# Products of ones in two waits of TensorE, and a residual that goes pair by pair, in a two-block transformer kernel

## The reference, cut to what matters

```python
h = rmsnorm(x, norm_pre_mix)
m = hgrn2_mixer(h, ...)                  # ends in the projection  o @ w_out
x = x + rmsnorm(m, norm_post_mix)        # the residual ahead of the FFN
h = rmsnorm(x, norm_pre_ffn)
x = x + rmsnorm(conv_ffn(h, ...), norm_post_ffn)
```

## Time and profile before

| what | value |
|---|---|
| median of 3 runs | 2503.98 us (2502.96 to 2504.39) |
| the profiled execution, first to last instruction | 2504.0 us |
| TensorE busy | 2480.6 us, 99% |
| VectorE, ScalarE, GpSimd busy | 1753.6, 1257.8, 29.5 us |
| mean granted clock of TensorE | 0.997 of full |
| HBM traffic | 463.5 MB, 185 GB/s over the span |

### The profile page before, as it was taken

How to read it: one execution, slowest core, us unless ns; L and a number is a source line. 1 busy time by engine, 2 the same in 40 slices (tenths; PEclk the granted TensorE clock), 3 DMA queues, 4 the chain that set the end, 5 groups by cost and what they waited for, 6 DMA issues and landing times.

```text
span 2504.0 us, 38061 instructions
## 1 busy us (share of the span) xinstructions
PE 2480.6 (99%) x15416; PEld 2115.6 (84%) x15416; DVE 1753.6 (70%) x1978; ACT 1257.8 (50%) x1506; POOL 29.5 (1%) x26
## 2 busy tenths in 40 slices
PE   9999999999999999999999999999999999999998
PEld 7888888888888888888888888888888888888886
DVE  6656765668668677675777777775776666777777
ACT  7655344544444444445555555544654444444543
POOL 0000000000000000000000000000000000000000
PEclk9999999999999999999999999999999999999999
DMA  9454545546546546555545454556465565556553
GB/s 381 153 183 152 176 153 193 176 164 223 193 161 231 187 171 211 193 195 183 185 153 185 153 185 153 185 170 195 150 217 185 186 200 187 183 194 198 186 188 127
DMA packets 128239, 465.97 MB, mean 186 GB/s; under 512 B 14368, under 2 KB 14624, under 8 KB 127168
## 3 DMA queue, kind: packets, MB, share of 16 engines
q1 hardware_dynamic: 127920, 463.53, 55.2%
q10 hardware_dynamic: 144, 0.02, 0.0%
HBM read 461.39 MB, written 2.10 MB: 185 GB/s over the span
## 4 chain that ended last, share of the span: by engine, by line
PE 94%; issue 4%; DVE 2%; ACT 0%; DMA 0%; SPq 0%; DVEq 0%; POOL 0%; POOLq 0%
PE job L970 30%; PE job L982 16%; PE job L938 11%; PE job L940 11%; PE job L939 11%; PE job L957 2%; PE job L958 2%; PE job L959 2%; PE att L958 2%; PE att L957 2%; PE att L959 2%; PE att L1177 1%; PE att L998 0%; DVE w_low L1593 0%; PE att L1010 0%
## 5 line engine op out<-in xcount | busy, mean ns | idle before, releaser
L1274 ACT ACTIVATE w_high<-raw 128x1024 fp32r<-128x1024 f32 (+1 forms) x883 | 919.6, 1050 | 733.9 <-PE job L940 292.4
L1593 DVE TENSOR_TENSOR w_low<-raw,w_high 128x1024 fp32r<-128x1024 f32 (+1 forms) x883 | 1047.0, 1212 | 310.5 <-ACT w_high L1274 231.0
L970 PE MATMUL job<-actA,w_high 128*128 128x512 f32 x3328 | 798.3, 391 | 0.1
L970 PEld LDWEIGHTS job<-actA,w_high 128*128 128x128 f32 x3328 | 611.8, 188 | 119.9 <-issue 0.7
L982 PEld LDWEIGHTS job<-actA,w_low 128*128 128x128 f32 x3328 | 426.7, 191 | 16.2
L982 PE MATMUL job<-actA,w_low 128*128 128x256 f32 x3328 | 431.7, 283 | 0.0
L1796 DVE TENSOR_TENSOR slots<-job,slots 128x512 f32<-128x512 f32 x102 | 70.5, 691 | 344.1 <-ACT slots L1466 343.5
L938 PE MATMUL job<-w_high,actB 128*128 128x512 f32 x736 | 288.6, 392 | 2.5 <-DVE w_low L1593 2.0
L939 PE MATMUL job<-w_low,actB 128*128 128x512 f32 x736 | 287.1, 390 | 0.0
L940 PE MATMUL job<-w_high,actB 128*128 128x512 f32 x736 | 287.0, 390 | 0.0
L938 PE MATMUL job<-w_high,actA 128*128 128x512 f32 x576 | 230.9, 401 | 0.0
(11 more groups left out here) (257 smaller groups left out, 1906.0 us busy)
## 6 DMA issues: line engine op xcount, KB each, us to landing
raw<-in_weights SPq DMA_DIRECT2D x855, 512.0 KB, 4.2
M<-in_mem_t SPq DMA_DIRECT2D x8, 256.0 KB, 8.0
slots<-in_mem SPq DMA_DIRECT2D x2, 1024.0 KB, 12.2
M<-in_x_t SPq DMA_DIRECT2D x4, 512.0 KB, 13.8
H<-in_x SPq DMA_DIRECT2D x2, 1024.0 KB, 9.0
out<-H SPq DMA_DIRECT2D x8, 256.0 KB, 3.2
slots<-in_w_small SPq DMA_DIRECT2D x1, 1024.0 KB, 9.7
slots<-in_post_mix_g SPq DMA_DIRECT2D x1, 1024.0 KB, 4.3
```

The lines of the kernel that those rows point to most:

```text
L970: mm = nc.tensor.matmul(J[job.buf][:, x, :], w_high[:, w % AHEAD, cols], act_both[job.act][:, c, :, :].rearrange("p a t -> p (a t)"), star ...
L1274: nc.scalar.activation(w_high[:, s % AHEAD, cols], raw[:, s % RAW_SLOTS, cols], ACT.Copy)\
L1593: nc.vector.tensor_tensor(w_low[:, s % AHEAD, cols], raw[:, s % RAW_SLOTS, cols], w_high[:, s % AHEAD, cols].bitcast(F32), ALU.subtract).t ...
```

## The change

It has three parts. (1) Behind window 0 TensorE does 8 more products of ones (fp32, 128x128), into a PSUM bank that nothing reads until it is written anew. (2) Behind window `end` it does 16 of them, ahead of `h_turn` 0. (3) The four steps from the residual to the FFN's activations are ordered pair by pair: step k does `post_add`, `h_turn` and `h_split` of pieces 2k and 2k+1, where before `post_add` and `h_turn` ran up to two pairs ahead of `h_split`. `m_gain` of quarter 3 moves from step `end + 2` to `end + 3`.

```diff
+FILL = {"second load": 8, "mixer norm": 16}
...
     p.put_early(end, "post_stat")
+    p.put_early(end, "fill", "mixer norm")
-    for step, added, split in ((end, range(0, 4), (0, 1)), (end + 1, (4, 5), (2, 3)), (end + 2, (6, 7), (4, 5)),
-                               (end + 3, (), (6, 7))):
-        if step == end + 2:
+    for step, added, split in ((end, (0, 1), (0, 1)), (end + 1, (2, 3), (2, 3)), (end + 2, (4, 5), (4, 5)),
+                               (end + 3, (6, 7), (6, 7))):
+        if step == end + 3:
             p.put_early(step, "m_gain", j.buf, 3)
...
                     products(w, range(TT)).then_inc(window_done, 1)
+                    if w == 0:
+                        fill("second load")
...
+            def fill(where):
+                for _ in range(FILL[where]):
+                    nc.tensor.matmul(att[:, 3, 0:P], ones[:, :], ones[:, :], start=True, stop=True)
...
+                elif name == "fill":
+                    for kind in ("o_low", "attended", "o_ready"):
+                        wait(pe, n, kind, 0)
+                    fill(*args)
```

More of the change, by code:

```diff
@@ L213 @@
     "hgrn_attend": dict(attended=1),
+    "fill": {},
     "m_part": dict(m_set=1),
```

## The result

The changed kernel takes 2510.13 us (median of 9 runs, 2509.68 to 2511.69), the kernel before 2503.98 us (median of 9). The ratio is 1.0025, with a 95% interval from 1.0016 to 1.0033: 6.15 us slower. The forecast was 2509.7 us, slower, and the new order as the cause. The time is right to 0.4 us, but by luck: two terms of its sum, of 1.6 us each and with opposite signs, stand for falls of the clock that need not be in the median execution, and they cancel.

The account below looks back on a forecast made before the run. The prediction took VectorE to bound the norm, with TensorE following. It summed 2504.0 - 1.6 (second load) + 5.7 (new order) + 1.6 (one fall in the new waits) = 2509.7 us, range 2507.4 to 2512.9.

Parts of the forecast that it names:

- two terms of its sum: Clock terms: -1.6 us for the fall removed at the second load, +1.6 us for one fall in the new waits.
- What bounds the norm: From 1756.4 to 1771.3 us VectorE, not TensorE, works without a gap, and TensorE follows.
- the walk: Step-by-step timing of pieces through VectorE, TensorE and ScalarE at the norm, at full clock: F3's narrow products 5.7 us later.
- The rival in which TensorE bounds the norm: VectorE's order counts for nothing and both fills win a whole fall: 2500.8 us; 5%.
- The new order, +5.7 us: Pair-by-pair order at the norm starts F3's narrow products at 1778.3 against 1772.55: +5.7 us, second fill's gain included.
- Products at the norm: Sixteen products inside TensorE's wait cost nothing at full clock; worth 0.2 us in the old order, within the +5.7 otherwise.
- Products at the second load, -1.6 us: Eight products behind window 0 fill TensorE's wait at no cost and prevent a clock fall: -1.6 us.
- the prediction's upper bound: At the second load, products at half clock would end 1.4 us late: +1.4 us, put aside.
- the rival: First fill wins nothing as the median execution's fall is elsewhere or escaped: 2511.3 us with one new fall; 7%.
- Falls in the new waits, +1.6 us: Five new TensorE waits at the norm bring one clock fall: +1.6 us, bounds 0 and 4.8.

Follow-up runs that it names:

- e3: Both runs of products of ones added to the kernel before, old order of the residual kept: 2504.27 us, ratio 1.0001.
- e10: Only the 16 products of ones at the norm added to the kernel before, old order: 2503.29 us, ratio 0.9997.
- e6: Changed kernel with residual and turns of pieces 4 and 5 put back a step earlier: 2506.92 us, ratio 1.0009 to the kernel before.
- e7: Both runs of products of ones on the kernel before, old order but for the first pair: 2505.86 us, ratio 1.0005.
- e4: Changed kernel plus 24 more products of ones in TensorE's new waits: 2510.4 us, ratio 1.0025 to the kernel before.
- the 3rd trace of the changed kernel: Another profiled execution of the changed kernel, nothing altered: time 2509.13 us, span 2507.3 us.
- e2: Only the new order on the kernel before, no products of ones: 2512.1 us, ratio 1.0033.
- its 2nd and 3rd trace: Two more profiled executions of the kernel before, nothing altered: times 2503.08 and 2503.73 us, spans 2501.3 and 2501.9 us.
- e1: Only the 8 products of ones behind window 0 added to the kernel before: 2504.39 us, ratio 1.0002.
- e9: Another profiled execution of e1, nothing altered: time 2504.21 us, span 2502.4 us.

## Why the prediction was right, and where it was not

**What bounds the norm**: right. VectorE does, shown by e3 and e10 (the fall at the norm taken away, the norm 19.13 and 19.14 us against 19.16) and by e6 and e7, in which only the order of VectorE's and TensorE's steps differs and the norm moves as the walk says. In the new order no single engine is busy throughout: the chain from engine to engine is the bound, and VectorE idles 6.2 us in it. The rival in which TensorE bounds the norm is out.

**The new order, +5.7 us**: right in size and step by step. At full clock it measures +5.69 (e4, and the 3rd trace of the changed kernel). The waits of the wide products and of turn 6 are in the places named: 1.29, 1.50, 1.49, 0.76 and 1.14 us, where the walk has 1.3, 1.5, 1.65, 0.9 and 1.3. (The prediction calls these "1.0 to 1.8 us"; its own times give 0.9 to 1.65.)

**Products at the norm**: right in the old order, nothing to win (e10). Left unpriced by itself in the new order, where it is the part of the change that pays: 1.9 us of norm between e2 and a trace at full clock, and 2512.1 us of e2 against 2510.13. The expectation for e2 gave it 0.3.

**Products at the second load, -1.6 us**: wrong at the median, by a premise that stands in the sum and ahead of the prediction too. "The profiled execution is the median run to 0.1 us" compared a span with times. The time is about 1.8 us more than its span, so the profiled execution was 1.8 us above the median, and what set it apart was the very fall that I then counted as won. Of five profiles without these products (before, its 2nd and 3rd trace, e2, e10) one has the costly fall there, one an earlier and cheaper one, three none. What took the term's place is nought, or up to 1.1 us of loss. The step behind it, that the products cost nothing, failed as well: they end behind the low part of window 1 in six of nine traces, at full clock (11.54 against 11.03 in the changed kernel). The loss by half clock, the prediction's upper bound, is not shown, since all nine profiles with these products had the full clock behind window 0. The Trainium skill, "TensorE: Matmul & The Clock Gate", section "What's actually happening", says that the same kernel meets the clock gate at another phase from run to run. The traces agree: of three executions of the kernel before, one has the fall behind window 1's first products, one in window 0, and one has none there. The prediction cited this and gave the rival 7%.

**Falls in the new waits, +1.6 us**: the mechanism is right and the place too; the price of one is 1.6 us, as said (norm 26.21 against 24.85, and 0.25 more behind it, where the rest is 731.72 against 731.47 us). It comes in two of three profiles, and not in e2, which has the same waits. How much of it is in the median is open, and the record points both ways. The median time of 2510.13 us is a span of 2508.3. With the fall that leaves a start of 2508.3 - 731.7 - 26.2 = 1750.4 us, earlier than in any of the fourteen traces (1750.71 at the least); without it 1751.95, well among them. And e4, whose profile has no fall, is no faster at the median. By this the median execution goes without the whole price. Yet the mean granted clock is 0.998 in seven of nine executions of the changed kernel, and 0.999 in 7 of 8 of e4 and in 10 of 11 of e3. That speaks for falls in most, though e7's profile, with no fall behind the start, reads 0.998 as well. Falls that lie partly in a wait, and so cost less, would fit both; no trace shows one.

**The sum.** With the right anchor it reads: 2504.0, 0 to +0.3 for the products at the load, +5.7 for the order, and a few tenths at most for falls, against the 2504.0 - 1.6 + 5.7 + 1.6 on record. The number was right by luck, since the two terms of the clock cancelled; the direction and the cause were not luck. Had I taken away only the first error, I would have said 2511.3.

## What to carry to other kernels

Ahead of any term made from one profiled execution, set that execution's time, not its span, beside the median, and look at a second trace before an event that may come by chance is counted as won. Where pieces pass through several engines, in-order engines need the next pair's first steps ahead of the last pair's last steps; the walk through a handful of measured hand-offs gives the price of undoing that to 0.1 us. Products of ones in a wait pay only if TensorE is what the following stretch waits for: at the norm they win nothing in the old order (19.14 against 19.16 us) and 1.9 us in the new one. And they have to end before the shortest wait that executions show, not the one of a single trace, or they hold up what follows, as at the second load.

## What the runs showed of the hardware

The same wait of 1.14 us ahead of F3 was followed by 1.2 GHz in two executions and by 2.4 GHz in two others (the 3rd trace of the changed kernel, and e2), and waits of 1.0, 1.2, 1.7 and 2.0 us at the second load by one fall, in the last. The fall within window 0 came behind a wait of 1.81 us. At the norm the wait of 3.8 us that was not filled with products was followed by half clock in six executions of six (before, its 2nd and 3rd trace, e1, e2, e9), from 0.7 us before TensorE resumed to 0.1 us behind it. The time behind the norm repeats to 0.1 us from trace to trace, 731.4 to 731.5 us, but for the one whose fall reaches into it, 731.7. What differs between executions of one kernel is the first 12 us, the falls, and up to 1.2 us more between window 1 and window `end`.
